# Column sums of squares in a two-block transformer kernel: squares stream through four column tiles instead of standing in the array

## The reference, cut to what matters

```python
y = x32 * lax.rsqrt(jnp.mean(x32 * x32, axis=-1, keepdims=True) + RMS_EPS)
h = y * w
proj = h @ w_in          # 1024 x 4356, then split into 15 parts
```

## Time and profile before

| | |
|---|---|
| time, median of 3 runs | 901.94 us (900.82 to 901.98) |
| the profiled execution | 900.98 us, span of its profile 899.7 us |
| busy in the span | PE 855.5 us (95%), DVE 416.4 (46%), ACT 302.0 (34%), POOL 10.3 (1%) |
| mean granted clock of TensorE | 0.989 of full speed |
| HBM read | 290 MB, 324 GB/s over the span |

### The profile page before, as it was taken

How to read it: one execution, slowest core, us unless ns; L and a number is a source line. 1 busy time by engine, 2 the same in 40 slices (tenths; PEclk the granted TensorE clock), 3 DMA queues, 4 the chain that set the end, 5 groups by cost and what they waited for, 6 DMA issues and landing times.

```text
span 899.7 us, 12205 instructions
## 1 busy us (share of the span) xinstructions
PE 855.5 (95%) x5030; PEld 554.2 (62%) x5030; DVE 416.4 (46%) x814; ACT 302.0 (34%) x548; POOL 10.3 (1%) x14
## 2 busy tenths in 40 slices
PE   5999999999998989899989899999999999999997
PEld 3668875344454334444444243489978999897985
DVE  3196964011210112001111011089898888989875
ACT  4253133111111111101111011174746666566663
POOL 0001000000000000000000000000100000010000
PEclk9999999999999999999999999999999999999999
DMA  9999989999999999999999999963425444653432
GB/s 371 424 428 427 402 351 428 410 428 428 427 429 428 426 428 427 428 426 428 428 428 427 428 422 423 402 245 123 168 86 187 142 164 180 180 154 105 179 141 71
DMA packets 34857, 292.96 MB, mean 326 GB/s; under 512 B 11376, under 2 KB 11888, under 8 KB 12912
## 3 DMA queue, kind: packets, MB, share of 16 engines
q1 hardware_dynamic: 34800, 292.16, 79.5%
HBM read 290.05 MB, written 1.05 MB: 324 GB/s over the span
## 4 chain that ended last, share of the span: by engine, by line
PE 71%; DMA 24%; DVE 3%; ACT 1%; SPq 1%; issue 1%; ACTq 0%
PE bank L1494 20%; PE bank L1042 16%; DMA more<-in_expert_w 14%; PE bank L1073 8%; DMA ring<-in_expert_w 7%; PE bank L1518 5%; PE bank L409 3%; DMA ring<-in_ada_w 3%; PE bank L1537 2%; PE bank L972 2%; DVE X L379 2%; PE bank L1013 2%; PE bank L452 2%; PE bank L425 1%; PE bank L1694 1%; PE bank L1720 1%
## 5 line engine op out<-in xcount | busy, mean ns | idle before, releaser
L1042 PE MATMUL bank<-ring,xg 128*64 128x512 f32 x760 | 234.5, 605 | 12.8 <-DMA ring<-in_expert_w 12.8
L1494 PE MATMUL bank<-HH,halves 128*128 128x256 f32 x848 | 164.0, 289 | 0.0
L1042 PEld LDWEIGHTS bank<-ring,xg 128*64 128x64 f32 x760 | 76.6, 139 | 123.1 <-issue 98.4
L1494 PEld LDWEIGHTS bank<-HH,halves 128*128 128x128 f32 x848 | 135.4, 192 | 4.6 <-issue 3.5
L1042 PE MATMUL bank<-more,xg 128*64 128x512 f32 x256 | 118.1, 614 | 7.5 <-DMA more<-in_expert_w 7.5
L1494 PE MATMUL bank<-HL,halves 128*128 128x256 f32 x424 | 120.3, 284 | 0.0
L1073 PE MATMUL bank<-ring,X 128*64 128x512 f32 x384 | 114.3, 595 | 0.7 <-ACT X L1113 0.7
L1160 DVE TENSOR_TENSOR X<-X,bank 128x512 f32<-128x512 f32 x16 | 11.0, 688 | 224.2 <-PE bank L1042 224.2
L1384 DVE TENSOR_TENSOR halves<-raw,halves 128x1024 fp32r<-128x1024 f32 (+1 forms) x84 | 91.9, 1128 | 6.4 <-ACT halves L1376 6.3
L1173 DVE SCALAR_TENSOR_TENSOR ygL<-bank,small,ygH 128x512 fp32r<-128x512 f32 x32 | 24.0, 750 | 136.2 <-ACT ygH L1120 136.2
L1494 PEld LDWEIGHTS bank<-HL,halves 128*128 128x128 f32 x424 | 81.6, 193 | 0.8 <-issue 0.5
(11 more groups left out here) (369 smaller groups left out, 1217.9 us busy)
## 6 DMA issues: line engine op xcount, KB each, us to landing
ring<-in_expert_w SPq DMA_DIRECT2D x63, 2048.0 KB, 26.9
more<-in_expert_w SPq DMA_DIRECT2D x22, 2048.0 KB, 26.2
raw<-in_units SPq DMA_DIRECT2D x38, 1024.0 KB, 4.9
ring<-in_ada_w SPq DMA_DIRECT2D x10, 2048.0 KB, 20.9
ring<-in_expert_w SPq DMA_DIRECT2D x17, 1024.0 KB, 28.1
ring<-in_w_in SPq DMA_DIRECT2D x3, 2048.0 KB, 34.7
more<-in_ada_w SPq DMA_DIRECT2D x2, 2048.0 KB, 27.7
ring<-in_w_out SPq DMA_DIRECT2D x2, 2048.0 KB, 22.0
```

Of the source, the lines that this page charges most:

```text
L1042: t = pe.matmul(bank[3 + i][64 * x:64 * x + 64, :], xg[q % 2][:, k, o + 64 * x:o + 64 * x + 64], w[:, k, :], start=k == 0, stop=k == 7)
L1494: t = pe.matmul(ps[:, T * j:T * j + T], part(x[:, k, 128 * j:128 * j + 128]), part(y[:, k, :]), start=first and a == 0, stop=last and a == ...
```

## The change

In both layers the squares become the moving operand. `square_parts` moves each chunk of squares (128 x 256) past a stationary operand of 32 columns, `crep[:, k, :]`, in column tile k mod 4: 8 products in layer 0, 4 in layer 1. The first column of the stationary operand is 1/1024, the second is `final_g` squared over 1024, the other 30 are zero. So a bank then holds four partial sums, in rows 0, 32, 64 and 96 (and 1, 33, 65, 97), with tokens along the row. ScalarE copies that 128 x 256 block to SBUF (`square_copy`, into `X1`), and `square_sums` makes it the stationary operand, 128 tokens at a time, of two products with `same_column` (1 where the partition modulo 32 is 0, and a second column for 1): this adds the four parts and gives the means with tokens on partitions, as before. ScalarE's root now waits for that second step.

The order on TensorE: in layer 0 six chunks of the pair, `square_parts`, one chunk, `square_sums`, one chunk, `tile(0, 2, 0)`, and only then `spread_pe` (it was ahead of that tile). In layer 1 four chunks, `square_parts`, two chunks, `square_sums`, two chunks, `spread_pe`, and then the tile as before.

`crep` held the conditioning vector for the first block's products. It is filled anew in `sums_dve`, five small VectorE instructions inside the first expert's work; two small ones at the start of the kernel go. The semaphore `s_cv` is folded into `s_xp`.

```diff
...
@@ -228,7 +228,7 @@
         E6, E5 = small[:, 300:301], small[:, 301:302]
         gw = small[:, 304:312]
 
-        sums = small[:, 218:234].rearrange("p (k c) -> p k c", k=8)
+        same_column = small[:, 218:220]
         cs = small[:, 0:8]
         s1 = small[:, 8:16]
         spl = [small[:, 16 + 4 * i:20 + 4 * i] for i in range(6)]
@@ -608,7 +608,7 @@
                 act.activation(xp[:, j, 3:3 + T], bank[4 + j // 2][:, T * (j % 2):T * (j % 2) + T], ACT.Copy).then_inc(s_xp, 1)
             for j in range(4):
                 act.wait_ge(s_xp, j + 1)
-                act.activation(xc[:, j, :], xp[:, j, 3:3 + T], ACT.Identity, bias=col("cb", j), scale=col("cw", 12 + j)).then_inc(s_cv, 1)
+                act.activation(xc[:, j, :], xp[:, j, 3:3 + T], ACT.Identity, bias=col("cb", j), scale=col("cw", 12 + j)).then_inc(s_xp, 1)
             for i in range(2):
                 act.wait_ge(s_proj, 3 + i)
                 act.activation(gv[:, i, :], bank[6 + i][:, :], ACT.Gelu_apprx_tanh, accum_out=vs[i]).then_inc(s_gv, 1)
@@ -702,8 +702,6 @@
             dve.wait_ge(s_cst, 16)
             for k in range(8):
                 dve.tensor_scalar(crep[:, k, :], con("one", 0, 32), cs[:, k:k + 1], None, ALU.mult).then_inc(s_gw, 1)
-            dve.memset(sums[:, :, 0], 1 / 1024).then_inc(s_gw, 1)
-            dve.scalar_tensor_tensor(sums[:, :, 1], col("fg", 0, 8), 1 / 1024, col("fg", 0, 8), ALU.mult, ALU.mult).then_inc(s_gw, 1)
             dve.wait_ge(s_root, 1)
             dve.reciprocal(rstd[:, :], rt[:, :]).then_inc(s_rstd, 1)
             dve.wait_ge(s_x, 16)
@@ -731,7 +729,7 @@
                     dve.tensor_scalar(spl[4], spl[2], 8.0, None, ALU.mult).then_inc(s_spl, 1)
                     dve.tensor_scalar(spl[5], spl[2], -8.0, None, ALU.mult).then_inc(s_spl, 1)
             for j in range(4):
-                dve.wait_ge(s_cv, j + 1)
+                dve.wait_ge(s_xp, j + 5)
                 for i, tap in enumerate((2, 1, 0)):
                     if i:
                         dve.wait_ge(s_conv, 3 * j + i)
@@ -1148,6 +1146,15 @@
                 dve.scalar_tensor_tensor(xT[:, m, :], bank[ACC[a]][:, T * k:T * k + T], modc[:, 40 + m:41 + m],
                                          xT[:, m, :], ALU.mult, ALU.add).then_inc(s_add, 1)
 
+        def sums_dve():
+
+            dve.wait_ge(s_mod, 6)
+            dve.memset(crep[:, :, :], 0.0).then_inc(s_gw, 1)
+            dve.wait_ge(s_gw, 10)
+            dve.memset(crep[:, :, 0], 1 / 1024).then_inc(s_gw, 1)
+            dve.scalar_tensor_tensor(crep[:, :, 1], col("fg", 0, 8), 1 / 1024, col("fg", 0, 8), ALU.mult, ALU.mult).then_inc(s_gw, 1)
+            dve.tensor_reduce(same_column, ident.rearrange("p (q r) -> p r q", q=4)[:, 0:2, :], AX, ALU.add).then_inc(s_gw, 1)
+
         def experts_dve(first, last):
             for n in range(first, last):
                 if n % 2 == 0 and n // 2 + 1 < NP // 2:
@@ -1163,6 +1170,7 @@
                 if n == 0:
                     modc_dve(10)
                     modc_dve(11)
+                    sums_dve()
                 dve.wait_ge(s_pg, n + 1)
                 if n >= 2:
                     dve.wait_ge(s_sct, 4 * (n - 1))
@@ -1552,23 +1560,30 @@
                                 t.then_inc(s_unit, 1)
                         yield
 
-                def sum_squares(ps, k, weights):
-
-                    n = weights.shape[1]
+                def square_parts(l):
+
+                    ps = bank[6] if l else bank[7]
+                    if l:
+                        pe.wait_ge(s_aXT, 8)
+                    else:
+                        pe.wait_ge(s_gw, 13)
+                    for n, k in enumerate((0, 1, 6, 7) if l else range(8)):
+                        if l:
+                            pe.wait_ge(*((s_sqx, 14) if n < 2 else (s_sqy, 4)))
+                        else:
+                            pe.wait_ge(s_sqx, 8 + k // 2 + 1)
+                        o = 32 * (n % 4)
+                        t = pe.matmul(ps[o:o + 32, 0:T], crep[:, 7 if l else k, :], squares[:, k, :], start=n < 4, stop=bool(l) or n >= 4,
+                                      tile_position=(0, o))
+                    t.then_inc(s_st2, 1)
+
+                def square_sums(l):
+
+                    ps, n = (bank[6], 1) if l else (bank[7], 2)
+                    pe.wait_ge(s_spart, l + 1)
                     for i in range(2):
-                        t = pe.matmul(ps[:, n * i:n * i + n], squares[:, k, 128 * i:128 * i + 128], weights, start=k == 0 and i == 0,
-                                      stop=k == 7, skip_group_check=True)
-                    return t
-
-                def stats(l, signal, value, rows):
-
-                    if rows[0] == 0:
-                        pe.wait_ge(s_aXT, 8 * l + 8)
-                    pe.wait_ge(signal, value)
-                    for k in rows:
-                        t = sum_squares(bank[6], k, con("ones", 0, 1))
-                    if rows[-1] == 7:
-                        t.then_inc(s_st2, 1)
+                        t = pe.matmul(ps[:, n * i:n * i + n], X1[:, 0, 128 * i:128 * i + 128], same_column[:, 0:n], start=True, stop=True)
+                    t.then_inc(s_st2, 1)
 
                 def spread_pe(value, half):
 
@@ -1730,24 +1745,17 @@
 
                 for l in range(2):
                     both = pair(l, 0, range(8), 2, h_ready(l))
+                    take(both, 4 if l else 6)
+                    square_parts(l)
+                    take(both, 2 if l else 1)
+                    square_sums(l)
+                    take(both, 2 if l else 1)
                     if l:
-                        take(both, 4)
-                        stats(0, s_sqx, 14, (0, 1))
-                        stats(0, s_sqy, 4, (6, 7))
-                        take(both, 4)
-                    else:
-                        take(both, 6)
-                        pe.wait_ge(s_gw, 11)
-                        for k in range(8):
-                            pe.wait_ge(s_sqx, 8 + k // 2 + 1)
-                            t = sum_squares(bank[7], k, sums[:, k, :])
-                            if k == 1:
-                                take(both, 1)
-                        t.then_inc(s_st2, 1)
-                        take(both, 1)
-                    spread_pe(11 if l else 6, 0)
+                        spread_pe(11, 0)
                     pe.wait_ge(s_hl, 8 * l + 8)
                     tile(l, 2, 0)
+                    if l == 0:
+                        spread_pe(6, 0)
                     tile(l, U_CO, 0)
                     tile(l, U_CO, 1)
                     values = by_token(l, U_BV)
@@ -1824,6 +1832,10 @@
                         tile(l, 21, 1, late)
 
             def second_act():
+                def square_copy(l):
+                    act.wait_ge(s_st2, 2 * l + 1)
+                    act.activation(X1[:, 0, 0:T], (bank[6] if l else bank[7])[:, 0:T], ACT.Copy).then_inc(s_spart, 1)
+
                 def scale_root(means, signal, value):
                     act.wait_ge(signal, value)
                     act.activation(root, means, ACT.Sqrt, bias=E6).then_inc(s_rt2, 1)
@@ -1924,7 +1936,8 @@
                 for l in range(2):
                     if l == 0:
                         high(l, 3)
-                        scale_root(bank[7][:, 0:4:2], s_st2, 1)
+                        square_copy(l)
+                        scale_root(bank[7][:, 0:4:2], s_st2, 2)
                         scale_root(mean, s_rs, 3)
                         high(l, 5)
                     else:
@@ -1933,7 +1946,8 @@
                         x_high(1, 6)
                         x_high(1, 7)
                         high(l, 2)
-                        scale_root(bank[6][:, 0:2], s_st2, 2)
+                        square_copy(l)
+                        scale_root(bank[6][:, 0:2], s_st2, 4)
                         high(l, 5)
                     gate_start(l)
                     if l == 0:
```

More of the change, by code:

```diff
@@ L196, in build @@
         s_mod, s_mrow, s_fma, s_turn, s_modc = (sem("s_" + n) for n in ("mod", "mrow", "fma", "turn", "modc"))
-        s_spl, s_proj, s_fill, s_xp, s_cv, s_conv, s_gv, s_ln, s_lnroot, s_sig, s_a, s_aa, s_lru = (
-            sem("s_" + n) for n in ("spl", "proj", "fill", "xp", "cv", "conv", "gv", "ln", "lnroot", "sig", "a", "aa", "lru"))
+        s_spl, s_proj, s_fill, s_xp, s_conv, s_gv, s_ln, s_lnroot, s_sig, s_a, s_aa, s_lru = (
+            sem("s_" + n) for n in ("spl", "proj", "fill", "xp", "conv", "gv", "ln", "lnroot", "sig", "a", "aa", "lru"))
         s_gr, s_scan, s_sgu, s_xres = (sem("s_" + n) for n in ("gr", "scan", "sgu", "xres"))
@@ L205, in build @@
                                     "down", "ygh", "ygl", "sct", "add"))
-        s_hi, s_lo, s_hh, s_hl, s_unit, s_sqx, s_sqy, s_st2, s_rt2, s_rs, s_rcT, s_xs = (
-            sem("s_" + n) for n in ("hi", "lo", "hh", "hl", "unit", "sqx", "sqy", "st2", "rt2", "rs", "rcT", "xs"))
```

(2 more changed lines are left out.)

## The result

| | before | after |
|---|---|---|
| time, median | 902.27 us (19 runs, 900.16 to 903.58) | 903.76 us (19 runs, 902.66 to 905.0) |
| ratio, 95% interval | | 1.002, 1.0013 to 1.0026 |
| the profiled execution | 900.98 us, span 899.7 | 902.83 us, span 901.5 |
| mean granted clock | 0.989 | 0.991 |
| TensorE busy | 855.5 us | 852.1 us |

The change makes the kernel slower by 0.2%, 1.2 to 2.3 us, though TensorE is drawn busy for 3.4 us less. The forecast was 904.2, and slower by over 0.2% (above 903.74) with a chance of 0.63. The median came at 903.76, 0.4 us under the forecast and just at that border; the measurement can't tell which side of it the kernel is on.

What follows compares the result with a forecast made beforehand. VectorE's list from its copy of the scales on was taken to set the time. Layer 0's +0.4 and layer 1's +1.95 gave +2.35 us, 903.3 for the profiled execution, forecast 904.2; range 901.6 to 906.2.

Steps and rivals of the forecast that it cites:

- Layer 0: First layer's sums: copy of the scales +0.7 us, less VectorE's 0.29 us wait behind it; net +0.4 us.
- layer 1, layer 1: Second layer's sums: means 2.25 us later delay ScalarE's root, VectorE's transposes and copy of the scales; +1.95 us.
- the copy of the scales: Line 2229 on VectorE, in both layers: its start sets the time, and a later copy delays all behind it.
- The slack that I read on TensorE in layer 1: Behind norm_mean, TensorE was read as already waiting 0.34 us for VectorE, hidden under drawn matmuls.
- the 0.29 of the wait: Layer 0, behind the copy of the scales: VectorE's 0.29 us wait for the gate rows' tile goes.
- the forecast's bound of +1.0: Layer 0's upper bound, +1.0 us, if the old kernel's clock didn't fall in other executions.
- What was taken as nothing: sums_dve in the first expert (at most 3.1 us uncovered), two removed small instructions and the folded semaphore: no effect.
- estimate for such a drain: TensorE's array mode switches: 0.16 us each, two a layer, would add 0.2 to 0.3 us; not taken.
- TensorE sets the time: Rival, chance 0.12: all TensorE savings count, 2.4 us in layer 0 and 0.7 in layer 1; 898.8 us.
- Only half arrives: Rival, chance 0.15: layer 1's 1.95 us is taken up before line 1677, layer 0's 0.4 stays; 902.3 us.
- The clock falls again: Rival, chance 0.08: TensorE's added waits bring another clock drop, up to 1.6 us on top; 905.8 us.
- The tiles don't run side by side: Rival, chance 0.03: the four column tiles run serially in both layers, +2.6 us more; 906.8 us.

Runs made afterwards that it cites:

- e1: Changed kernel with layer 0 back to the old 2-column sums and early spread, so only layer 1 changed; 903.94 us, +2.1 us against the kernel before.
- e5: Kernel before with two more 128 x 256 copies on VectorE right ahead of its copy of the scales in each layer; 902.77 us, +1.0 us against before.
- e9: Changed kernel with layer 1's two added products (square_sums) one chunk sooner, spread in place; 902.55 us, +0.9 us against the kernel before.
- e11: Changed kernel with layer 0's spread ahead of the gate rows' tile again, layer 1 untouched; 902.59 us, +0.7 us against the kernel before.
- e10: Kernel before with 6 of 24 half products of tile(l, U_CO, 0) left out in each layer; 902.06 us, +0.5 us against before.
- e6: Kernel before with six more 256-column products on TensorE at the start of unit 3 in each layer; 903.03 us, +0.6 us against before.
- e7: Kernel before with only layer 1's four transposes on VectorE moved ahead of its wait for the scale; 901.70 us, -0.8 us against before.
- e2: Changed kernel with layer 1 as in the kernel before, so only layer 0 changed; 902.16 us, -0.2 us against the kernel before.
- e3: Changed kernel with layer 1's four transposes on VectorE moved ahead of its wait for the scale's root; 901.53 us, -0.5 us against the kernel before.
- e4: Changed kernel with layer 1's transposes ahead of the root wait and layer 0's spread ahead of the gate rows' tile; 900.65 us, -2.0 us against before.
- e8: As e3, with layer 0's sums right behind the parts, then chunk, spread, chunk, tile; 899.87 us, -2.0 us against the kernel before.

## Why the prediction was right

*The sum.* For an execution like the profiled one 903.3 was forecast (+2.35 us), and 902.83 came (+1.85). Layer 0 (A + B) gave +0.07 where +0.4 was said, layer 1 (C + D) +1.80 where +1.95 was said, and the rest of the span -0.05.

*What bounds the kernel.* That the copy of the scales sets the time, and not the TensorE chain that the page draws with 71%, held: e1, e5 and e9 move the copy of layer 1 and e11 that of layer 0, and all behind it moves with it, within 0.13 us; e10 takes work from TensorE and moves nothing in layer 1. The Trainium skill says in "Perfetto Trace Analysis", section "Tensor Engine Instruction (MATMUL, LD_WEIGHTS)", that the profiler estimates a matmul's end and does not observe it. The trace agrees: in the earlier trace rows line 1677's pair is drawn for 1.10 to 1.12 us, whether the next product starts 1.14, 0.90 or 0.56 us behind it. The slack that I read on TensorE in layer 1 (0.34 us, from the earlier trace rows) was wrong for the other sign: e6 shows about 0.1. The forecast didn't use it, since TensorE got less work and not more.

*Layer 0.* The spread was forecast at 606.45 and starts at 606.44; the copy at 607.1, and starts at 607.07. The parts take 2.15 us, since they wait for VectorE's squares; their end at 600.23 was forecast at 600.1. Two terms behind the copy were mis-sized. From the copy to the gate rows it is 2.80 us for 3.17 before, 0.37 less where I took the 0.29 of the wait. And a pause of 0.22 us between two VectorE instructions at 653.3 in the profile before is missing in the one after. VectorE's timelines, before and below it after:

```profile
652.81 0.42 DVE L2099 TENSOR_TENSOR scr<-scr,late 128x256 f32<-128x256 f32 x1
653.36 0.43 DVE L2103 TENSOR_TENSOR scr<-scr 128x256 f32<-128x256 f32 x1
```

```profile
653.09 0.42 DVE L2113 TENSOR_TENSOR scr<-scr,late 128x256 f32<-128x256 f32 x1
653.42 0.42 DVE L2117 TENSOR_TENSOR scr<-scr 128x256 f32<-128x256 f32 x1
```

The pause stands in all four profiles whose VectorE list up to there is that of the kernel before (that kernel, e6, e7, e10) and in none of the ten with more VectorE instructions ahead of it (e5 among them, whose sums are the old ones). So it goes with the place in VectorE's list and not with the sums; what makes it isn't shown. 0.66 - 0.37 - 0.22 = 0.07. That layer 0 came out near zero is in part luck.

Layer 0 holds a loss and, in some executions, a gain. The loss is the moved spread: e11 puts it back, and A goes from 10.02 to 8.35. The gain is the clock: of six profiles with the old sums in layer 0, three show the 1.2 GHz level behind them (the kernel before, e1, e7: A = 9.33 to 9.50), and three don't (e5, whose first added copy starts at 8.82, e6 at 8.82 and e10 at 8.83). So a fall costs A 0.5 to 0.7 us (0.6 was the forecast's price for it), and against an old kernel without one the copy of the changed one is 1.2 us later, not 0.7. A + B is 63.32 in the changed kernel, and 62.44 (e10) and 62.91 (e6) in old ones without a fall, whose TensorE has 0.73 us less and more to do: +0.4 to +0.9, inside the forecast's bound of +1.0 for this case. How many executions of the kernel before have the fall isn't known; over the runs as they came, e2 shows -1.0 to +0.7 us. The forecast took it that the new sums never have it. Of eight profiles with them none does, against three of six; if the kind of sums made no difference, the three would all lie among the six by chance in one case of 18. So that is likely, and not shown.

*Layer 1.* The root was forecast at 753.9 and starts at 754.03; the transposes were to end at 759.95, and the copy starts at 759.96, with no wait for the spread, which starts at 756.80, three microseconds sooner. The copy is 1.97 us later than the earlier trace rows (forecast 1.95). In D, 0.12 us come back, nearly all at once: the step from the copy to the gate rows is 0.11 us shorter. e3 fills the gap with the transposes and e9 makes it smaller, and each takes away as much as the gap allowed; so this cause is shown, not argued.

*What was taken as nothing.* `sums_dve` is four VectorE instructions and not five, from 156.53 to 157.00 us, and VectorE's wait behind them, is 0.55 us shorter after, so they are hidden there:

```profile
161.66 0.75 DVE L1181 SCALAR_TENSOR_TENSOR ygL<-bank,small,ygH 128x512 fp32r<-128x512 f32 x1 [4.25 <-ACT ygH L1118]
```

VectorE's first square starts at 597.07 before and 597.05 after. That alone says little, since this start varies with the execution: from 597.0 to 598.4 us in the nine profiles with `sums_dve` and from 597.1 to 598.9 in the five without. ScalarE's copy takes 0.39 us (0.40 forecast).

*Array shape.* The Trainium skill says in "TensorEngine Tiling (Array Packing)", "Key Properties", that a change of the mode drains TensorE. The prediction's estimate for such a drain, 0.16 us each from the drawn length, would have added 0.2 to 0.3 us to the sum. TensorE's timeline in layer 1 after:

```profile
749.74 0.28 PE L1502 MATMUL bank<-HH,halves 128*128 128x256 f32 x1
749.95 0.64 PE L1576 MATMUL bank<-scr,crep 128*32 128x256 f32 x8
750.52 0.38 PE L1502 MATMUL bank<-HH,halves 128*128 128x256 f32 x1
750.74 0.28 PE L1502 MATMUL bank<-HL,halves 128*128 128x256 f32 x1
```

Going in costs 0.21 - 0.12 = 0.09 us as in the earlier trace rows, the four tiles 0.57 for 0.48, and the first full product behind them 0.22 for 0.12: about 0.28 us for both ways, where I had put in 0.1 (leaving taken as free) and two drains would be 0.32. So the estimate by a drain had the better size for this term, whether or not the cause is one, which no run here tells. In the root's start only 0.13 us of it is left, since the added products took less than forecast, 0.36 us (753.50 to 753.86) for 0.43.

*The rivals.* "TensorE sets the time" fails by e10: 1.46 us less work for it gain 0.4 us at most. "Only half arrives" fails: of 1.92 us, 1.80 arrive. (Its price, 902.3, has nothing of layer 1 in it, so it stood for less than half.) "The clock falls again": none of the eight profiles with the new sums in layer 0 shows less than full clock from 600 to 613 us, nor any of the fourteen between 744 and 764. "The tiles don't run side by side" fails: four products take 0.57 us, where one behind the other they would take four times 0.48. (The prediction priced this rival with 0.43 us a product, for which it shows no row; with the 0.48 of the earlier trace rows it would have been 907.5.)

*The version that is better.* The changed sums with both delays taken away (e4) take 900.65 us, 2.0 us under the kernel before. So the column tiles were worth something, and the two places in the order where the changed kernel loses time cost more than that: from the changed kernel to e4 it is 3.8 us. e8 reaches the same.

## What to carry to other kernels

Where a change takes work off the engine that the chain shows, look first at who waits for whom at the next meeting point, by the distance between starts: if that engine already waits there, the result is set by when the change lets the other engine go on. A result that takes an extra hop (parts, copy, sums) comes later even if it costs less, and the first thing to do about it is to fill the waiting engine's gap with work that it has anyway, here the four transposes, worth 2.4 us. Slack read at one meeting point holds for that point alone: 0.73 us more on TensorE in layer 1 went round it through ScalarE.

## What the runs showed of the hardware

A fall of the clock behind the 2-column products comes in some executions and not in others. The three profiles with the fall are those in which VectorE's first square starts at 596.99 to 597.16 us; in the three with the same products and no fall it starts at 598.32 to 598.87. But five profiles with the new sums start at 597.04 to 597.27 and show no fall. The granted clock was 0.53 in the stretch of the earlier trace rows, 0.52 in a stretch of e1 (603.0 to 606.5 us), and in e7 it stood at 0.50 up to 611. Six profiles are few, and the start of the square need not be the cause: anything else that shifts between executions may separate them as well. What decides it, and why the start differs by over 1 us between executions, isn't shown.

Four fp32 products of 256 columns in four column tiles took 0.57 us in layer 1, against an estimate of 0.48 us for one by itself (a quarter of the 1.92 us of the earlier trace rows); going in and coming back cost 0.09 and 0.10 us beside the usual distance of 0.12.
